# Seven of eight feed-forward blocks: the down projection as seven half-size products (one level of Strassen's identity)

## The chip, the cores and the metric

The kernel runs on one core of a Trainium2 chip. The metric is the time of one execution on the device in microseconds (us). Engines: TensorE (PE; PEld is its weight load), VectorE (DVE), ScalarE (ACT), GpSimd (POOL), and SyncE (SP), whose queue issues the DMAs.

## What is computed

Two layers of a decoder on 1056 tokens (1024 of a prompt, 32 of a sample group), model width 1024, all in FP32. The part that matters here is the feed-forward network at the end of each layer:

```python
hf = einsum('btd,df->btf', rmsnorm(x, norm_ffn_pre), w_up)        # 1024 -> 4096
f  = einsum('btf,fd->btd', square(relu(hf)), w_down)              # 4096 -> 1024
x  = x + rmsnorm(f, norm_ffn_post)
```

Before it stand an input projection, latent attention, chunked spatial gating and an output projection.

## The kernel before, in words

Tokens lie along the free dimension: every activation is a set of tiles of 128 channels x 1056 tokens. A projection is computed in FP32R with both operands split in a high part (rounded to FP32R) and a low part (the remainder), in three passes: high x high, high weights x low activations, low weights x high activations. `dense` (L1660 to L1674) computes one unit of 128 output channels: for each k tile of 128 input channels and each pass, three matmuls of 352 columns, one per group of tokens, into three PSUM banks. Units alternate between banks 0 to 2 and 3 to 5; banks 6 and 7 hold means.

The FFN of a layer runs in FB = 8 blocks of 512 hidden channels. A block has four up units (`up`, 8 k tiles each, 72 matmuls) and eight down units (`down`, and `down_first` for units 0 and 1, whose matmuls stand at L2144; 4 k tiles each, 36 matmuls). Weights come as tiles of 128 x 1024 numbers (512 KB): one for each up unit, one for two down units. The path of a tile is:

- SP loads it into `raw[:, t % 2]` (L559), once the tile two before it has been split (`split`).
- POOL splits it (`split_tile`): L605 writes the high part `wh`, L607 subtracts it and writes the low part `wl`. It waits for `wfree`, by which PE gives a slot back with the first matmul of the next tile. There are two slots.
- PE waits for `split` and runs the tile's matmuls.

The path of the activations in a block: DVE evicts an up unit with relu and the norm's root (L1526), ACT squares it (L1017) and writes the high part `hidh` (L1019), DVE writes the low part `hidl` (L1519). PE's down units read these, and DVE adds each down unit to the running sum in `z[:, m]` (L1552, in the first block a copy, L1550). `acc_full` and `acc_free` tie PE and DVE, `hid_h` and `hid_l` the hidden tiles. Each engine's order is the order of its own program: nothing is scheduled. The first block of a layer and the last stand apart; those between run in a hardware loop.

The last block ends in a special order (L1701), by token groups, so that the norm can begin early.

## Time and profile before

| | us |
|---|---|
| median of 3 runs | 2690.55 (2690.33 to 2691.85) |
| the profiled execution | 2691.78 |
| its span, first to last instruction | 2690.0 |
| PE busy in the span | 2608.7 (97%) |
| DVE busy | 1104.4 (41%) |
| POOL busy | 768.5 (29%) |
| ACT busy | 684.1 (25%) |

Busy time is the time in which an engine has an instruction under way. Matmuls overlap in it: a matmul's recorded duration (some 323 ns for 352 columns) is longer than the spacing of matmuls, which is what their number in a stretch gives. "Idle before" is the time that an engine stood still before the instructions of a group, with what ended it.

### The profile page before, as it was taken

Reading aid. Unit: us, or ns where it says so; the run is one execution under the profiler, and the core shown is the slowest. Engines: PE = TensorE matmul, PEld = TensorE weight load, DVE = VectorE, ACT = ScalarE, POOL = GpSimd, SP = SyncE. Lnnn points to the kernel's source line nnn. Section 1 sums busy time; section 2 is a strip of 40 time slices with the busy share of each in tenths; the row PEclk is TensorE's granted clock in tenths of the full one; section 3 lists DMA queues with packets and bytes.
Section 4 is the critical chain, followed back from the end, with each engine's and each line's share of the span. In section 5 each row is a group of like instructions: output and inputs, shape, how many; then the busy total and the mean of one; then the engine's idle time right before and its main releaser. Section 6 shows DMA issues by size and latency. Waiting matters only on the chain.

```text
span 2690.0 us, 42193 instructions
## 1 busy us (share of the span) xinstructions
PE 2608.7 (97%) x17128; PEld 2363.6 (88%) x17128; DVE 1104.4 (41%) x1519; ACT 684.1 (25%) x1151; POOL 768.5 (29%) x363
## 2 busy tenths in 40 slices
PE   8999999999999999999999999999999999999996
PEld 6995666979999999999879866669799999999996
DVE  5456666254212222322664566652732123212226
ACT  3125555141100110010341255551411000100113
POOL 2431000313334433443114300003043334433440
PEclk9999999999999999999999999999999999999998
DMA  6114222221111111111231242213211111111113
GB/s 220 48 38 128 80 80 72 112 88 40 48 47 47 39 47 47 47 42 44 112 112 40 52 125 81 85 54 120 81 48 48 47 47 41 45 47 47 47 40 137
DMA packets 91492, 185.97 MB, mean 69 GB/s; under 512 B 29664, under 2 KB 42144, under 8 KB 91360
## 3 DMA queue, kind: packets, MB, share of 16 engines
q1 hardware_dynamic: 88656, 175.75, 19.7%
q0 software_dynamic: 2560, 8.39, 1.1%
q8 instruction: 91, 1.49, 0.2%
q14 instruction: 41, 0.34, 0.0%
q10 hardware_dynamic: 144, 0.00, 0.0%
HBM read 157.77 MB, written 23.11 MB: 67 GB/s over the span
## 4 chain that ended last, share of the span: by engine, by line
PE 86%; ACT 4%; DVE 4%; issue 4%; POOLq 1%; DVEq 0%; DMA 0%; POOL 0%; SPq 0%; ACTq 0%
PE psum L1671 54%; PE psum L2144 7%; PE psum L1861 3%; PE psum L1701 3%; PE psum L1887 3%; PE psum L1873 2%; PE psum L1656 2%; PE psum L1764 2%; PE psum L1908 2%; PE psum L1624 1%; ACT z L863 1%; ACT hh L734 1%; PE psum L1921 1%; PE psum L1940 1%; PE psum L1919 1%
## 5 line engine op out<-in xcount | busy, mean ns | idle before, releaser
L605 POOL TENSOR_TENSOR wh<-raw,ones 128x1024 fp32r<-128x1024 f32 x150 | 288.4, 1923 | 1274.3 <-PE psum L1671 1096.3
L1671 PE MATMUL psum<-hh,wh 128*128 128x352 f32 x2064 | 448.6, 325 | 0.0
L1671 PE MATMUL psum<-hh,wl 128*128 128x352 f32 x2064 | 444.8, 323 | 0.0
L1671 PE MATMUL psum<-hl,wh 128*128 128x352 f32 x2064 | 444.3, 323 | 0.0
L607 POOL TENSOR_TENSOR wl<-raw,wh 128x1024 fp32r<-128x1024 f32 x150 | 413.7, 2758 | 21.7
L1017 ACT ACTIVATE z<-z 128x1056 f32<-128x1056 f32 x64 | 69.7, 1089 | 1221.0 <-DVE stat L1530 1199.5
L1671 PEld LDWEIGHTS psum<-hh,wl 128*128 128x128 f32 x2064 | 354.3, 188 | 0.0
L1671 PEld LDWEIGHTS psum<-hh,wh 128*128 128x128 f32 x2064 | 351.8, 189 | 2.5 <-issue 0.6
L1671 PEld LDWEIGHTS psum<-hl,wh 128*128 128x128 f32 x2064 | 350.4, 188 | 0.0
L1526 DVE SCALAR_TENSOR_TENSOR z<-psum,rinv 128x1056 f32<-128x1056 f32 x64 | 80.5, 1258 | 549.6 <-PE psum L1671 542.2
L1552 DVE TENSOR_TENSOR z<-psum,z 128x1056 f32<-128x1056 f32 x104 | 130.8, 1258 | 392.2 <-PE psum L1671 339.3
L1671 PE MATMUL psum<-hidh,wh 128*128 128x352 f32 x1056 | 228.4, 324 | 0.0
L1671 PE MATMUL psum<-hidh,wl 128*128 128x352 f32 x1056 | 227.6, 323 | 0.0
L1671 PE MATMUL psum<-hidl,wh 128*128 128x352 f32 x1056 | 227.4, 323 | 0.0
L1671 PEld LDWEIGHTS psum<-hidh,wl 128*128 128x128 f32 x1056 | 181.4, 188 | 0.0
L1671 PEld LDWEIGHTS psum<-hidh,wh 128*128 128x128 f32 x1056 | 179.9, 189 | 0.0
L1671 PEld LDWEIGHTS psum<-hidl,wh 128*128 128x128 f32 x1056 | 179.3, 188 | 0.0
L628 POOL DMA_INDIRECT z<-cache_k,krows x32 | 30.5, 952 | 395.1 <-DVE cn L1381 390.9
L1519 DVE TENSOR_TENSOR hidl<-z,hidh 128x1056 fp32r<-128x1056 f32 x64 | 129.4, 2022 | 11.9 <-ACT hidh L1019 11.3
L863 ACT ACTIVATE z<-psum,stat 128x128 f32<-128x128 f32 (+7 forms) x128 | 94.7, 740 | 73.0 <-DVE stat L1345 70.5
L1128 DVE TENSOR_TENSOR sacc<-sacc,t 128x1056 f32<-128x1056 f32 x45 | 67.7, 1505 | 104.3 <-ACT t L976 89.7
L1345 DVE TENSOR_REDUCE stat<-psum 128x1 f32<-128x128 f32 (+7 forms) x128 | 95.9, 750 | 14.5 <-PE psum L1864 13.3
(242 smaller groups left out, 3564.8 us busy)
## 6 DMA issues: line engine op xcount, KB each, us to landing
raw<-wst SPq DMA_DIRECT2D x160, 512.0 KB, 3.2
z<-cache_c SPq DMA_DIRECT2D x352, 64.0 KB, 1.8
x<-x_spill SPq DMA_DIRECT2D x4, 4224.0 KB, 14.3
raw<-cache_c SPq DMA_DIRECT2D x160, 64.0 KB, 1.8
x_spill<-x SPq DMA_DIRECT2D x2, 4224.0 KB, 13.4
x_spill<-x SPq DMA_DIRECT2D x6, 1408.0 KB, 5.2
x<-xT SPq DMA_DIRECT2D x8, 528.0 KB, 8.1
yT<-x SPq DMA_DIRECT2D x6, 704.0 KB, 3.3
```

The lines of the kernel that those rows point to most:

```text
L605: pool.tensor_tensor(wh[:, s, :], raw[:, s, :], ones[:, 0:1].to_broadcast([P, TW]), ALU.mult)
L607: pool.tensor_tensor(wl[:, s, :], raw[:, s, :], wh[:, s, :].bitcast(F32), ALU.subtract).then_inc(split.sem, 1)
L863: act.activation(probs[e][:, 0:(j + 1) * P], s_of(e, j), ACT.Exp, bias=stat[:, 32 + e:33 + e], accum_out=stat[:, 36 + e:37 + e]).then_inc( ...
L1345: dve.tensor_reduce(stat[:, 32 + e:33 + e], s_of(e, j), AX.X, ALU.max, negate=True).then_inc(nmax.sem, 1)
L1519: dve.tensor_tensor(hidl[:, j, :], z[:, 10 + j % 2, :], hidh[:, j, :].bitcast(F32), ALU.subtract).then_inc(hid_l.sem, 1)
L1526: dve.scalar_tensor_tensor(out=groups(z[:, 8 + j % 2, :]), in0=acc(j), scalar=0.0, in1=groups(rinv[:, :]), op0=ALU.max, op1=ALU.mult).then ...
L1552: ins = dve.tensor_tensor(groups(z[:, m, :]), acc(m), groups(z[:, m, :]), ALU.add)
L1671: ins = pe.matmul(bank3(u, g), w[:, s, o:o + P], m[:, k, cols(g)], start=(k == 0 and n == 0), stop=(k == kk - 1 and n == 2))
L1701: ins = pe.matmul(bank, u_w[w], m[:, k, cols(g)], start=(first and n == 0), stop=(last and n == 2))
L1861: ins = pe.matmul(ps[2 * e + h][:, 0:w], qs[e][0:KQ, u, tok(j)], keys[0:KQ, 2 * (u % 2) + e, 512 * h:512 * h + w], start=True, stop=not last)
L1887: ins = pe.matmul(ps[6][64 * e:64 * e + 64, 0:P], vals[:, kb, (2 * u + e) * VD:(2 * u + e) * VD + VD], pts[2 * e + kb // 4][:, kb % 4, :], ...
L2144: ins = pe.matmul(bank3(u, g), w[:, 0, o:o + P], m[:, k, cols(g)], start=(k == 0 and n == 0), stop=(k == 3 and n == 2))
```

## The change

In blocks 0 to 6 of each layer the down projection is one level of Strassen's identity. The block's down weights (512 hidden x 1024 output channels) and its hidden activations (512 channels x 1056 tokens) are cut in quarters: 256 hidden channels, 512 output channels, 528 tokens. Seven products of a weight combination with an activation combination take the place of eight products of quarters. The last block stays as it was.

- **PE** (`downs`): for each of seven terms, four units of 128 output channels in the order 0, 3, 1, 2; for each 2 k tiles x 3 passes x 2 halves of 264 columns. Unit u has banks 2u and 2u + 1. The table `TERMS` says for each term which half of the output channels and tokens it goes to, and whether its banks start afresh (terms 0, 2 and 6) or chain on what the term before left in them. DVE adds the banks to `z` after every term, so a chained term goes on from the running combination; each unit of a term waits for the eviction of that unit in the term before (`dn_free`).
- **POOL** (`split_downs`): from the four quarters `a11`, `a12`, `a21`, `a22` it forms four sums and differences (L679, L672) and splits seven operands (L657, L659). The quarters lie in `t0`, `cn`, `sacc` and `t1`, and `s4` in the cosine table, all free in the FFN.
- **SP** (`downs_in`): eight transfers of 256 KB take the place of four of 512 KB; they wait for the last split of the block before. The cosine table is loaded anew during the last block of the first layer.
- **ACT and DVE** (`hidden_parts`, `parts_of`): ACT squares in place; DVE forms four differences of quarters (`less`, L1667); the high and low parts are made per quarter combination into four tiles of `hidh` and `hidl` (L1674), three of which are written a second time in a block. DVE evicts 28 half-size units (`take`, L1688 and L1690).

The core of the diff:

```diff
+SB = FB - 1
+N_UP, N_DN = 4, 7
+HB, HW = TOK // 2, TOK // 4
+TURN = (0, 3, 1, 2)
+TERMS = [(1, 3, True, (1, 1)), (2, 3, False, (0, 1)), (0, 0, True, (0, 0)), (3, 1, False, (0, 1)),
+         (1, 1, False, (1, 1)), (2, 1, False, (1, 0)), (0, 0, True, (0, 0))]
...
+                def downs_in(tile):
+
+                    for n, (left, right) in enumerate(((a11, a12), (a11, a12), (a21, a22), (a21, a22))):
+                        own = slice(TW // 2 * (n % 2), TW // 2 * (n % 2) + TW // 2)
+                        for j, slot in enumerate((left, right)):
+                            sp.dma_start(slot[:, own],
+                                         wst[l, tile + n][:, TW // 2 * j:TW // 2 * j + TW // 2]).then_inc(dn_in.sem, 16)
...
+                def split_downs(s):
+
+                    at.step(dn_in, 128)
+                    pool.wait_ge(dn_in.sem, at.value(dn_in))
+                    pool.tensor_tensor(a21, a21, a22, ALU.add)
+                    pool.drain()
+                    split_one(s, a21)
+                    combine(a21, a21, a11, ALU.subtract)
+                    combine(s4, a12, a21, ALU.subtract)
+                    split_one(1 - s, s4)
+                    split_one(s, a11)
+                    split_one(1 - s, a21)
+                    combine(a21, a22, a21, ALU.subtract)
+                    split_one(s, a21)
+                    split_one(1 - s, a22)
+                    split_one(s, a12)
...
+                def hidden_parts():
+
+                    squared(0)
+                    squared(1)
+                    act.drain()
+                    high_hid(0, slice(0, 2), b11)
+                    high_sum(1, 0, b12)
+                    for k in range(2):
+                        squared(2 + k)
+                        act.drain()
+                        high_hid(2, slice(k, k + 1), b22)
+                    high_sum(3, 0, b12)
+                    high_sum(1, 4, b11)
+                    high_sum(2, 8, b12)
+                    act.wait_ge(dn_full.sem, at.value(dn_full, 12))
+                    high_hid(0, slice(0, 2), b21)
...
+                    def take(f, units):
+
+                        for u in units:
+                            at.step(dn_full)
+                            dve.wait_ge(dn_full.sem, at.value(dn_full))
+                            outs_of = [TERMS[f][3]]
+                            for i, half in outs_of:
+                                part = quarter(4 * i + u, half)
+                                if first and (i, half, u) not in seen:
+                                    ins = dve.tensor_copy(part, dn_banks(u))
+                                else:
+                                    ins = dve.tensor_tensor(part, dn_banks(u), part, ALU.add)
+                                seen.add((i, half, u))
+                            ins.then_inc(dn_free.sem, 1)
+
+                    both = slice(0, 2)
+                    relu(0)
+                    relu(1)
...
+                    squares_done(2)
+                    less(b12, b12, b11)
+                    low(0, both, b11)
+                    low(1, both, b12)
+                    relu(2)
+                    low(2, slice(0, 1), b22)
+                    relu(3)
+                    low(2, slice(1, 2), b22)
+                    take(0, TURN[:2])
+                    squares_done(2)
+                    less(b12, b22, b12)
+                    take(0, TURN[2:])
+                    low(3, both, b12)
+                    take(1, TURN[:2])
+                    dve.drain()
+                    less(b11, b12, b11)
+                    take(1, TURN[2:])
+                    low(1, both, b11)
+                    take(2, TURN[:2])
+                    dve.drain()
+                    less(b12, b21, b12)
+                    take(2, TURN[2:])
+                    low(2, both, b12)
+                    take(3, TURN)
+                    low(0, both, b21)
+                    for f in range(4, 7):
+                        take(f, TURN)
...
+                def downs(flip):
+
+                    ready = (2, 4, 1, 5, 6, 7, 8)
+                    where = (1, 2, 0, 3, 1, 2, 0)
+                    for f in range(7):
+                        s, t, fresh = (f + flip) % 2, where[f], TERMS[f][2]
+                        take_tile()
+                        pe.wait_ge(hid_l.sem, at.value(hid_l, ready[f]))
+                        for u in TURN:
+                            if f:
+                                pe.wait_ge(dn_free.sem, at.value(dn_free, -3))
+                            elif u < 2:
+                                pe.wait_ge(acc_free.sem, at.value(acc_free, u - 1))
+                            at.step(dn_free)
+                            for k in range(2):
+                                o = u // 2 * 4 * P + k * 2 * P + u % 2 * P
+                                for n, (w, m) in enumerate(((wh, hidh), (wh, hidl), (wl, hidh))):
+                                    for q in range(2):
+                                        ins = pe.matmul(psum[:, 2 * u + q, 0:HW], w[:, s, o:o + P],
+                                                        m[:, t, k * HB + q * HW:k * HB + q * HW + HW],
+                                                        start=(fresh and k == 0 and n == 0), stop=(k == 1 and n == 2),
+                                                        skip_group_check=True)
+                                        release(ins)
+                            ins.then_inc(dn_full.sem, 1)
```

How the instructions stand, at the two places that matter. First VectorE, in the first block of a layer, from the last up unit's low half on. Before (`hidl` low parts, L1526 the relu, L1550 the evictions of the eight down units):

```order
L1519 TENSOR_TENSOR hidl<-z,hidh 128x1056 [waits hid_h]
L1526 SCALAR_TENSOR_TENSOR z<-psum,rinv 128x1056 [waits acc_full]
L1530 MEMSET stat 128x1
L1519 TENSOR_TENSOR hidl<-z,hidh 128x1056 [waits hid_h] x2
L1550 COPY z<-psum 128x1056 [waits acc_full] x8
```

After, the same place up to the end of the fourth term's evictions:

```order
L1674 TENSOR_TENSOR hidl<-z,hidh 128x528 [waits hid_h]
L1688 COPY z<-psum 128x528 [waits dn_full] x2
L1667 TENSOR_TENSOR z<-z 128x2x528 [waits h_sq]
L1688 COPY z<-psum 128x528 [waits dn_full] x2
L1674 TENSOR_TENSOR hidl<-z,hidh 128x1056 [waits hid_h]
L1688 COPY z<-psum 128x528 [waits dn_full] x2
L1667 TENSOR_TENSOR z<-z 128x2x528
L1688 COPY z<-psum 128x528 [waits dn_full] x2
L1674 TENSOR_TENSOR hidl<-z,hidh 128x1056 [waits hid_h]
```

The low parts and the differences now stand between the evictions for which PE waits; before, all low parts stood ahead of them.

Second GpSimd, in a block between the first and the last. Before (one tile of the loop; the down tiles are split in the same way):

```order
L603 ISA [waits raw_in0]
L605 TENSOR_TENSOR wh<-raw,ones 128x1024 [waits wfree]
L607 TENSOR_TENSOR wl<-raw,wh 128x1024
```

After, from the sum of two quarters to the split of the third operand (`t` is t0 or t1, `cos` holds `s4`):

```order
L679 TENSOR_TENSOR sacc<-sacc,t 128x1024 [waits dn_in]
L655 REGISTER_ALU
L657 TENSOR_TENSOR wh<-sacc,ones 128x1024 [waits wfree]
L659 TENSOR_TENSOR wl<-sacc,wh 128x1024
L672 TENSOR_TENSOR sacc<-sacc,t 128x1024
L672 TENSOR_TENSOR cos<-cn,sacc 128x1024
L655 REGISTER_ALU
L657 TENSOR_TENSOR wh<-cos,ones 128x1024 [waits wfree]
L659 TENSOR_TENSOR wl<-cos,wh 128x1024
L655 REGISTER_ALU
L657 TENSOR_TENSOR wh<-t,ones 128x1024 [waits wfree]
L659 TENSOR_TENSOR wl<-t,wh 128x1024
```

Sums and differences stand between the splits, on the same engine.

## Rows read from the trace of the kernel before

**Rows 1.** The page, busy us (share of the span) and instructions of each engine:

```profile
PE 2608.7 (97%) x17128; PEld 2363.6 (88%) x17128; DVE 1104.4 (41%) x1519; ACT 684.1 (25%) x1151; POOL 768.5 (29%) x363
```

**Rows 2.** Busy time by stretch, two FFN blocks; columns as in the first line:

```profile
core 0: us, PE busy (x) PEld busy (x) DVE busy (x) ACT busy (x) POOL busy (x), PEclk, DMA share, GB/s
1192.28:1285.47 93.19, 93.19 (x578) 93.19 (x577) 23.47 (x20) 8.72 (x8) 36.85 (x16) 1.00 0.13 45
1965.53:2058.72 93.19, 93.19 (x577) 93.19 (x577) 23.45 (x20) 8.71 (x8) 36.86 (x16) 1.00 0.13 46
```

**Rows 3.** The chain of waits: start us, us, what:

```profile
633.12 11.62 PE psum L2144 x72
644.74 81.57 PE psum L1671 x504
```

**Rows 4.** Waits, 633 to 1285 us: who waited for whom, us, times, longest:

```profile
POOL wh L605 <- PE psum L1671: 341.5, 49, 7.2
DVE z L1526 <- PE psum L1671: 262.4, 28, 10.4
```

**Rows 5.** PE groups by shape, FP32 matmuls of attention: busy us, mean ns:

```profile
L1861 PE MATMUL psum<-scratch,free_b 96*128 96x512 f32 x96 | 48.8, 593 | 0.0
...
L1861 PE MATMUL psum<-scratch,free_a 96*128 96x384 f32 x32 | 13.0, 486 | 0.0
...
L1861 PE MATMUL psum<-scratch,free_a 96*128 96x256 f32 x32 | 9.6, 380 | 0.0
...
L1861 PE MATMUL psum<-scratch,free_b 96*128 96x128 f32 x32 | 6.3, 277 | 0.0
```

**Rows 6.** PEld groups by shape, weight loads of 128 and 32 columns:

```profile
L1671 PEld LDWEIGHTS psum<-hidh,wl 128*128 128x128 f32 x1056 | 181.4, 188 | 0.0
...
L1919 PEld LDWEIGHTS psum<-z,sacc 128*32 128x32 f32 x256 | 5.0, 108 | 5.4 <-issue 4.1
```

**Rows 7.** Timeline of PE around an FP32R matmul of 128 columns (L1864):

```profile
271.68 0.39 PE L1861 MATMUL psum<-scratch,free_a 96*128 96x128 f32 x2
271.82 0.31 PE L1864 MATMUL psum<-trir,idr 128*128 128x128 f32 x1
271.96 0.52 PE L1908 MATMUL psum<-cst,z 128*128 128x128 f32 x3
```

**Rows 8.** DVE groups by shape, whole span, the last row for 633 to 1297 us:

```profile
L1552 DVE TENSOR_TENSOR z<-psum,z 128x1056 f32<-128x1056 f32 x104 | 130.8, 1258 | 392.2 <-PE psum L1671 339.3 <-PE psum L2144 52.9
...
L1374 DVE COPY z<-psum 128x512 f32<-128x512 f32 x32 | 22.0, 689 | 5.9 <-PE psum L1908 5.8
...
L1576 DVE TENSOR_TENSOR z<-psum,z 128x704 f32<-128x704 f32 x12 | 10.7, 890 | 8.3 <-PE psum L1701 8.3
...
L1519 DVE TENSOR_TENSOR hidl<-z,hidh 128x1056 fp32r<-128x1056 f32 x30 | 61.6, 2053 | 4.6 <-ACT hidh L1019 4.3
```

**Rows 9.** Timeline of DVE and POOL after the last up unit:

```profile
634.54 1.83 DVE L1519 TENSOR_TENSOR hidl<-z,hidh 128x1056 fp32r<-128x1056 f32 x1
636.91 2.83 DVE L1519 TENSOR_TENSOR hidl<-z,hidh 128x1056 fp32r<-128x1056 f32 x1 [0.54 <-ACT hidh L1019]
...
633.36 1.90 POOL L605 TENSOR_TENSOR wh<-raw,ones 128x1024 fp32r<-128x1024 f32 x1 [6.39 <-PE psum L2144]
635.40 3.23 POOL L607 TENSOR_TENSOR wl<-raw,wh 128x1024 fp32r<-128x1024 f32 x1
```

**Rows 10.** ACT groups by shape: the square, and a high part of 512 elements:

```profile
L1017 ACT ACTIVATE z<-z 128x1056 f32<-128x1056 f32 x64 | 69.7, 1089 | 1221.0 <-DVE stat L1530 1199.5 <-DVE hl L1163 21.5
...
L817 ACT ACTIVATE hh<-z 128x512 fp32r<-128x512 f32 x16 | 10.0, 627 | 18.4 <-POOL z L623 18.4
```

**Rows 11.** Timeline of POOL, a split with DVE elsewhere:

```profile
644.98 1.90 POOL L605 TENSOR_TENSOR wh<-raw,ones 128x1024 fp32r<-128x1024 f32 x1 [6.36 <-PE psum L1671]
647.02 2.40 POOL L607 TENSOR_TENSOR wl<-raw,wh 128x1024 fp32r<-128x1024 f32 x1
```

**Rows 12.** DMA issues: times, KB each, median us to landing:

```profile
raw<-wst SPq DMA_DIRECT2D x160, 512.0 KB, 3.2
```

More of the change, by code:

```diff
@@ new lines, in _ @@
+                at.step(split)
+                sp.wait_ge(root_full.sem, at.whole(root_full, 7))
+                downs_in(base + 4)
+                at.step(split, N_DN)
+                with sp.Fori(0, SB // 2) as i:
+                    at.enter(i, {split: 2 * (N_UP + N_DN)})
+                    for b in range(2):
+                        tile = i * 16 + (base + 8 + 8 * b)
+                        for j in range(2):
+                            up_in(tile + j, j, j - 8)
+                        sp.wait_ge(split.sem, at.value(split))
+                        downs_in(tile + 4)
+                        for j in range(2, 4):
+                            up_in(tile + j, j, j - 1)
+                        at.step(split, N_UP + N_DN)
+                    at.leave(SB // 2)
@@ L569, in _ @@
                 if l < DEPTH - 1:
-                    sp.wait_ge(hid_l.sem, at.whole(hid_l, 4 * FB))
+                    sp.wait_ge(hid_l.sem, at.whole(hid_l, hid_l.per))
                     for u in range(2):
@@ L666, in _ @@
                 taken_elsewhere()
-                split_tiles(TILES_LAYER - T_OUT - KD - 6)
+                at.step(split)
+                at.step(wfree)
+                split_downs(1)
+                with pool.Fori(0, SB // 2) as i:
+                    at.enter(i, {split: 22, wfree: 22, raw_in[0]: 64, raw_in[1]: 64, dn_in: 256})
+                    for b in range(2):
+                        for j in range(4):
+                            split_tile(j % 2, slot=(j + b) % 2)
+                        split_downs(b)
+                    at.leave(SB // 2)
+                split_tiles(6)
                 split_tile(0)
@@ L1516, in low, with block_of @@
+                def block_of(last):
                     def low(j):
@@ L1531, in block_of @@
                         at.step(act_new)
-                        if first and j == 1:
-                            low_h(range(EARLY, KD), gn[:, G_FFN_PRE:G_FFN_PRE + KD])
-                            low_w(1, at.whole(w_hi, 4))
-                            dve.drain()
                         if j > 0:
```

204 lines of the change are left out of this document (138 added, 66 removed).

## Prediction

> **What bounds the kernel now.** I read the page's shares first. TensorE is busy for 97% of the span, VectorE for 41%, GpSimd for 29% and ScalarE for 25% [rows 1]. Shares are means over stages, so the stretch that the change touches came next. Two FFN blocks, one of each layer, each take 93.19 us, PE busy in all of it, at a granted clock of 1.00, which is 2.4 GHz [rows 2]. The reader is to see there that PE never waits within a block, while POOL needs 36.9 us and DVE 23.4 us of it. The chain of waits says the same from the other side: for a whole block it names only matmuls of the dense loop and of the first down units [rows 3]. A block has 4 x 72 + 8 x 36 = 576 matmuls of 352 columns, so one costs 93.19 / 576 = 161.8 ns. The waits of the other engines confirm the direction: POOL waited 341.5 us for PE to give back a weight slot, and DVE 262.4 us for full accumulators [rows 4]. So only less PE time, or a new PE wait, can move the total. Seven blocks in each of two layers change: 14 blocks, and 1 us in a block is worth 14 us.
>
> **What PE saves.** The eight down units of a block go: 288 x 161.8 ns = 46.6 us. In their place stand seven products of 4 units x 2 k x 3 passes x 2 column halves = 48 matmuls of 264 columns, 336 in all. No row has a matmul of this type with 264 columns, so I bound it. In proportion to columns it costs 161.8 x 264 / 352 = 121.4 ns. If only the streaming part shrinks, at one column per cycle of 2.4 GHz (the granted clock is 1.00), 88 columns save 36.7 ns, which leaves 125.1 ns. That durations follow columns is seen in the plain FP32 matmuls of attention: 593, 486, 380 and 277 ns for 512, 384, 256 and 128 columns [rows 5], some 0.83 ns per column, which is two passes at 0.42. Against it stands that every matmul loads its own 128 x 128 weights. Loads of 128 and of 32 columns are recorded at 188 and 108 ns [rows 6], so 96 columns are worth 80 ns and 128 some 107 ns, just under the 110 ns that 264 columns stream. And around the one FP32R matmul of 128 columns, the next matmul begins 0.14 us after it [rows 7], so neither its stream nor its load holds the array for 162 ns. I take 123 ns: 41.3 us for the seven products, and 5.3 us less than before. The ends, 40.8 and 42.0 us, stay in the range.
>
> The Trainium skill, "TensorE: Matmul & The Clock Gate", section on the back-to-back issue gap, has a warm gap of N/2.4 + 2.5 ns. It gives 149 ns for 352 columns, which the trace contradicts (161.8 ns). By it 264 columns would take 112.5 ns, and the seven products 37.8 us.
>
> **What VectorE adds.** Evictions from PSUM grow from 8 of 1056 elements (1258 ns) to 28 of 528. Rows of 512 and 704 elements read 689 and 890 ns [rows 8], so one takes 0.71 us: 10.1 us become 19.8. New are four sums or differences of squared activations, and the low halves become seven of 1056 elements instead of four. The eviction reads one tensor from SBUF and never lengthens (1258 ns mean over 104). The low half reads two, and lengthens: 1.83 and 2.83 us [rows 9]. The reader is to lay its times beside POOL's. The first runs 634.54 to 636.37, POOL's product held 633.36 to 635.26: 1.11 us from there. The second ends 639.74, POOL's subtraction 638.63: 1.11 us again. POOL's subtraction started at 635.40 and took 3.23 us, where undisturbed ones take 2.40. So these operations exclude one another, each for its whole length. DVE's cost is 1.11 us plus what is left of POOL's operation.
>
> In the products of index 0, 1 and 2 DVE does four evictions (2.8 us), one difference and one low half (2 x 1.11 = 2.2 us), and waits twice for POOL. The waits are 0 at best and a full 1.72 us, as in the second case above, at worst. POOL's split holds 4.3 us of each 5.9 us product, so a random arrival waits 0.73 x 1.08 = 0.8 us. With 0.2 us of drains and hops a stage costs 2.8 + 2.2 + 1.6 + 0.2 = 6.8 us against PE's 48 x 123 ns = 5.9 us. PE cannot run ahead: unit u of a product waits for the eviction of unit u of the one before, because both chain in the same banks. Nor is there much slack at entry. After the last up unit DVE's relu takes 1.26 us, ACT's square and half-size copy 1.09 + 0.6 [rows 10], DVE's half-size low 0.6 + 0.8, hops 0.4: the first eviction ends at 5.5 us, and PE wants that bank at 5.9. So PE waits 3 x 0.9 - 0.4 = 2.3 us, and each of some five restarts exposes a weight load of 0.11 us: 2.9 us. I take 3.2, since POOL's margin, next, is thin. With no lock wait it is 0; with a full one each time it is near 3 x 2.7 = 8 us.
>
> **What GpSimd adds.** A split costs 1.90 + 2.40 us with a gap of 0.14 between them, 4.45 us [rows 11]. There were 8 in a block, now there are 11, and four sums of 2.4 us with a drain: 37 us become about 59, of some 91. It is hidden in the up units, where PE spends 11.6 us per tile. Among the products it is tight. From the start of the last up unit to the end of the last split POOL has 7 splits (31.2 us), three differences (7.7 us), and DVE's operations of two inputs in its way (7 to 8 x 1.11 = 8 us): 46.9 us. PE needs the last split after 11.6 + 6 x 5.9 = 47.0 us, and its own waits for DVE give POOL some 3 us more. I cost POOL at nothing on that ground.
>
> **Other edits.** ACT gains about 4 us per block on 8.7 and idles otherwise. DMA moves the same bytes: the down tiles come as eight transfers of 256 KB, issued on the SP queue after the last split of the block before. A tile of 512 KB lands in 3.2 us [rows 12]; four of them have over 20 us before POOL needs them, and the up tiles queued behind them over 10 us more. In the first block they start after the reciprocal root and have the two up units of 23.3 us. The cosine table's reload is hidden by the last block. The new order of the slots costs nothing.
>
> **The sum.** A block: 46.6 + 41.3 + 3.2 = 91.1 us against 93.2, 2.1 us less, times 14 = 29 us. The profiled execution took 2691.78 us (span 2690.0 and 1.8 around it), so it would take 2662.4; the median of the runs shown, 2690.55, lies 1.2 lower. Forecast: **2661 us**. Its own range is 2637 to 2680, for waits of 1.5 to 4.5 us in a block.
>
> **Rivals.**
> *Full gain.* DVE meets POOL rarely, since it can slip into POOL's drains; a stage then costs 5.3 us, under PE's 5.9. Block 87.9 us, 5.3 x 14 = 74 us less: 2616 us. For it: the lock lets DVE in after each POOL operation. Against: the 30 low halves of seven blocks take 2053 ns in the mean [rows 8], 0.9 us over 1.11, with POOL busy for 37 us of a block and not 59.
> *GpSimd becomes the bound (slower).* The place is the last split among the products. Each DVE operation costs POOL up to 1.11 us, and each POOL operation costs DVE the same; a late split also delays the next unit's eviction, so that the waits add up instead of overlapping. If POOL is 4 us late in a block besides the 3.2, the block is 95.1 us: 27 us more, 2717 us. It decides from 5.3 us of waits in all. For it: 46.9 us of work in a window of 47.0. Against: PE's waits for DVE widen that window.
> *A matmul of 264 columns costs what one of 352 does.* Something fixed per matmul, the weight load with its handover, sets the 161.8 ns. Then the products take 54.4 us, the waits vanish, a block is 101.0 us: 109 us more, 2800 us. The point of decision is 139 ns, 46.6 us / 336. Against: [rows 5 to 7]. For: nothing here has this type at 264 columns, and 161.8 is 15 ns above 352 columns at 2.4 GHz, unexplained.
> The same section of the skill's TensorE page has a sustained gap of about 81 ns at 128 columns and 131 ns at 512, 0.13 ns per column. By it 88 columns save 11 ns only, a product's matmul costs 150 ns, and the result is 2745 us; no row here bears it out, and rows 5 speak against it.
> That the change does less than it says I leave out: the instruction order has the 336 matmuls of 264 columns.
>
> **How the numbers follow.** Forecast 0.59, full gain 0.13, GpSimd 0.20, fixed matmul cost 0.08. About 0.2% (5 us) is what a measurement of this kernel can tell from no change. Of the forecast's case 0.05 falls within it. Faster: 0.54 + 0.13 = 0.67; same 0.05; slower 0.28. The range leaves out the fixed cost, a tail above the GpSimd case and a little below the full gain: 2614 to 2725.
>
> **What would show it.** Right: matmuls of 264 columns spaced 121 to 125 ns; in each block PE waits for DVE's evictions, mostly in the products of index 1 to 4, and hardly in 5 and 6; DVE's two-input operations at 1.9 us and more in the mean; POOL's subtraction often over 2.4 us. Wrong: waits of PE for POOL's split above 1 us per block (the slower rival), no waits (full gain), a spacing above 139 ns, or a wait for a DMA at the sum of the two left quarters.

## The result, and the profile after

| | before | after |
|---|---|---|
| median, us | 2691.07 (4 runs) | 2716.24 (4 runs, 2711.61 to 2721.42) |
| the profiled execution | 2691.78 | 2716.44 |
| its span | 2690.0 | 2714.6 |

The change makes the kernel slower by 0.9%: the ratio is 1.0093, 95% interval 1.0081 to 1.0105. The forecast was 2661 us. The page of the changed kernel, busy us (share) and instructions, against [rows 1]:

```profile
PE 2557.4 (94%) x17800; PEld 2301.6 (85%) x17800; DVE 1451.4 (53%) x1911; ACT 730.5 (27%) x1207; POOL 1141.3 (42%) x503
```

PE has 51 us less to do and the span is 25 us longer. So PE stands still, or goes slower, where it did neither before. Two whole blocks, one of each layer, as in [rows 2]:

```profile
core 0: us, PE busy (x) PEld busy (x) DVE busy (x) ACT busy (x) POOL busy (x), PEclk, DMA share, GB/s
1154.83:1247.14 92.31, 88.52 (x627) 87.69 (x625) 47.98 (x48) 12.07 (x12) 62.96 (x26) 1.00 0.11 36
2021.57:2113.88 92.31, 88.48 (x626) 87.65 (x625) 47.98 (x48) 12.06 (x12) 62.95 (x26) 1.00 0.15 47
```

These blocks are faster than 93.19 us, but by 0.88 us only: if all fourteen were like them, 14 x 0.88 = 12.3 us in all. The profiled execution is 24.7 us slower, so 37 us have to be explained by what such an undisturbed block does not show. What PE waited for (waiting engine and line, releaser, us in total, times, longest):

```profile
PE psum L2360 <- POOL wl L659: 51.4, 36, 2.7
PE psum L1879 <- issue: 20.6, 6, 4.9
```

The first row is a wait within the block: products (L2360) for a split by GpSimd (L659). The second is new in kind: at up units (L1879) PE stood still six times for 20.6 us, and no tile was late. [Rows 3] of before have neither. For VectorE's evictions, where the prediction looked for the waits, PE waited twice, 1.1 us.

**Within the block.** The chain of waits from 1200 to 1230 us, the stretch from the last up unit to the end of product 3, by line:

```profile
by line: POOLq L658 32.9%; POOL wl L659 26.5%; POOLq L673 18.9%; issue 16.6%; POOLq L671 10.9%; PE psum L2360 1.7%; POOLq L655 0.5%
```

It is GpSimd's. Its timeline there (start us, us, line, operation; in brackets its idle time and who ended it):

```profile
1201.80 1.90 POOL L657 TENSOR_TENSOR wh<-cos,ones 128x1024 fp32r<-128x1024 f32 x1 [1.76 <-PE psum L2360]
1203.84 2.40 POOL L659 TENSOR_TENSOR wl<-cos,wh 128x1024 fp32r<-128x1024 f32 x1
1207.95 3.01 POOL L657 TENSOR_TENSOR wh<-t,ones 128x1024 fp32r<-128x1024 f32 x1 [1.71 <-PE psum L2360]
1211.10 3.22 POOL L659 TENSOR_TENSOR wl<-t,wh 128x1024 fp32r<-128x1024 f32 x1
1215.01 2.18 POOL L657 TENSOR_TENSOR wh<-sacc,ones 128x1024 fp32r<-128x1024 f32 x1 [0.69 <-PE psum L2360]
1217.33 3.24 POOL L659 TENSOR_TENSOR wl<-sacc,wh 128x1024 fp32r<-128x1024 f32 x1
1220.73 3.24 POOL L672 TENSOR_TENSOR sacc<-t,sacc 128x1024 f32<-128x1024 f32 x1 [0.16 <-issue]
1224.17 2.66 POOL L657 TENSOR_TENSOR wh<-sacc,ones 128x1024 fp32r<-128x1024 f32 x1 [0.20 <-issue]
1226.98 2.34 POOL L659 TENSOR_TENSOR wl<-sacc,wh 128x1024 fp32r<-128x1024 f32 x1
```

Two things are to be seen. GpSimd is idle for 1.76, 1.71 and 0.69 us, each time until PE begins another product: there are two slots, and a split may not begin before PE has left one. And of the seven operations that follow the first two, six are longer than in [rows 11]: 3.01, 2.18 and 2.66 for 1.90 us, 3.22 and twice 3.24 for 2.40 us, where VectorE's two-input operations fall beside them. So the split for product 2 begins behind PE's start of product 1 and takes 6.4 us, where a product takes 5.8. The split for product 4 stands behind a difference, and ends at 1229.32. The timeline of PE has the first matmuls of products 2 and 4:

```profile
1214.55 0.51 PE L2360 MATMUL psum<-hidh,wh 128*128 128x264 f32 x2 [0.95 <-POOL wl L659]
...
1229.54 0.51 PE L2360 MATMUL psum<-hidh,wh 128*128 128x264 f32 x2 [2.66 <-POOL wl L659]
```

VectorE's two-input groups and evictions by shape (busy us, mean ns), against [rows 8]:

```profile
L1690 DVE TENSOR_TENSOR z<-psum,z 128x528 f32<-128x528 f32 x360 | 244.4, 701 | 137.7 <-PE psum L2360 133.6 <-issue 3.9
...
L1674 DVE TENSOR_TENSOR hidl<-z,hidh 128x1056 fp32r<-128x1056 f32 x84 | 174.5, 2091 | 2.2 <-issue 2.0
L1667 DVE TENSOR_TENSOR z<-z 128x1056 f32<-128x1056 f32 x56 | 117.5, 2097 | 18.4 <-ACT z L1117 15.9
```

The evictions wait 133.6 us for PE, not PE for them. Their rhythm in product 6 gives the price of a matmul (timeline of DVE):

```profile
1240.06 0.71 DVE L1690 TENSOR_TENSOR z<-psum,z 128x528 f32<-128x528 f32 x1 [0.75 <-PE psum L2360]
...
1247.34 0.71 DVE L1690 TENSOR_TENSOR z<-psum,z 128x528 f32<-128x528 f32 x1 [0.75 <-PE psum L2360]
```

Five units of 12 matmuls in 7.28 us: 121.3 ns, in proportion to the columns. Seven products would take 40.8 us; from 1201.43 to 1247.14 they take 45.7 us. So 4.9 us of the block are waits and restarts. PE's waits for GpSimd's splits are 51.4 / 14 = 3.7 us of them.

**At the jump.** PE's hardware loop (L2414) holds two blocks now: a block has 4 + 7 = 11 tiles, an odd number, so the two slots change places from one block to the next. The loop runs three times and jumps back twice per layer. The timeline of PE and of SP's queue around one jump:

```profile
865.04 0.40 PE L2360 MATMUL psum<-hidh,wl 128*128 128x264 f32 x2
...
870.31 1.24 PE L1879 MATMUL psum<-hh,wh 128*128 128x352 f32 x3 [4.87 <-issue]
...
858.62 0.33 SPq L592 DMA_DIRECT2D t<-wst  x1
...
863.39 0.33 SPq L592 DMA_DIRECT2D t<-wst  x1
864.44 11.54 SPq L585 DMA_DIRECT2D raw<-wst  x2
```

And busy time by stretch, columns as above:

```profile
865.20:870.30 5.10, 0.25 (x3) 0.03 (x1) 0.71 (x1) 0.00 (x0) 0.00 (x0) 0.97 0.73 249
...
846.10:849.50 3.40, 3.25 (x15) 3.25 (x16) 1.25 (x2) 0.00 (x0) 2.44 (x2) 0.50 0.00 0
849.60:853.00 3.40, 3.40 (x30) 3.40 (x29) 1.74 (x3) 0.00 (x0) 1.84 (x1) 1.00 0.00 0
...
869.97:873.37 3.40, 3.06 (x10) 3.06 (x11) 0.00 (x0) 0.00 (x0) 2.18 (x2) 0.50 0.04 11
```

The first row is the pause: PE has nothing, while the DMA engines are busy for 0.73 of it, mostly with the transfers of the down tiles. The six pauses of the row above are one at each of the four jumps (4.9, 4.4, 4.4 and 4.6 us) and a second one some 3 us behind the last two (1.6 and 0.8 us). The fetch of instructions goes on throughout the loop. From 650 to 1250 us the instruction queue moved, in the kernel before (packets, MB, share):

```profile
q8 instruction: 7, 0.11, 0.1%
```

And in the changed one:

```profile
q8 instruction: 36, 0.59, 0.4%
```

The other rows of the stretches show the third loss. In 3.40 us behind a wait at product 4, and in 3.40 us behind the pause, the granted clock is 0.50, the 1.2 GHz level: 15 matmuls where the next stretch at 1.00 has 30, so up to 1.7 us each. The fourteen blocks of this execution have ten stretches at half clock, 44 us in all, those of before none. What they cost can be read from whole blocks: from 2261.51 to 2355.34 and from 2456.15 to 2549.97 us stand two blocks with one stretch of 3.4 us and no pause, and they take 93.83 and 93.82 us where undisturbed ones take 92.31. That is 1.5 us each, so some 20 us for 44 us at half clock.

The sum of the profiled execution, read block by block: the fourteen blocks together take 28.2 us more than fourteen of 93.19 us, and the rest of the kernel 3.6 us less than before. The 28.2 us are -12.3 us from the faster products, +20.6 us from the pauses at the jump, and 19.9 us that are left for the half clock, and agree with the price just read. Outside the blocks the half clock stood for some 15 us less than before, which can account for the 3.6 us.

### The profile page after: what moved, and what is told of

Read it like the earlier page. It is cut to its first block, busy times and chain, and to the rows that moved or that the text cites. A ratio compares the mean times of both kernels' runs of the same rounds, so it can differ in the third digit from the quotient of the medians.

```text
span 2714.6 us, 44972 instructions
## 1 busy us (share of the span) xinstructions
PE 2557.4 (94%) x17800; PEld 2301.6 (85%) x17800; DVE 1451.4 (53%) x1911; ACT 730.5 (27%) x1207; POOL 1141.3 (42%) x503
## 4 chain that ended last, share of the span: by engine, by line
PE 37%; issue 26%; POOLq 21%; POOL 7%; ACT 3%; DVE 3%; DMA 1%; SPq 1%; DVEq 0%; ACTq 0%
PE psum L1879 13%; POOLq L658 12%; POOL wl L659 7%; POOLq L673 4%; PE psum L2069 3%; POOLq L671 3%; PE psum L2095 3%; PE psum L2081 2%; PE psum L1909 2%; POOLq L680 2%; PE psum L1864 2%; PE psum L1972 2%; PE psum L2116 2%; PE psum L2360 1%; PE psum L1832 1%
## 5 line engine op out<-in xcount | busy, mean ns | idle before, releaser
L1879 PE MATMUL psum<-hh,wh 128*128 128x352 f32 x2064 | 452.4, 328 | 18.2 <-issue 18.2
L657 POOL TENSOR_TENSOR wh<-raw,ones 128x1024 fp32r<-128x1024 f32 x94 | 182.1, 1937 | 651.2 <-PE psum L1879 542.6
L1879 PE MATMUL psum<-hh,wl 128*128 128x352 f32 x2064 | 447.9, 325 | 2.4 <-issue 2.4
L1879 PE MATMUL psum<-hl,wh 128*128 128x352 f32 x2064 | 446.9, 325 | 0.0
L2360 PE MATMUL psum<-hidh,wh 128*128 128x264 f32 x1568 | 328.3, 291 | 53.9 <-POOL wl L659 51.4
L1879 PEld LDWEIGHTS psum<-hh,wh 128*128 128x128 f32 x2064 | 354.4, 190 | 21.2 <-issue 19.0
L1879 PEld LDWEIGHTS psum<-hh,wl 128*128 128x128 f32 x2064 | 356.5, 189 | 3.3 <-issue 3.3
L1879 PEld LDWEIGHTS psum<-hl,wh 128*128 128x128 f32 x2064 | 352.8, 189 | 0.0
L2360 PE MATMUL psum<-hidl,wh 128*128 128x264 f32 x1568 | 322.1, 287 | 0.0
L2360 PE MATMUL psum<-hidh,wl 128*128 128x264 f32 x1568 | 321.9, 287 | 0.0
L1690 DVE TENSOR_TENSOR z<-psum,z 128x528 f32<-128x528 f32 x360 | 244.4, 701 | 137.7 <-PE psum L2360 133.6
L2360 PEld LDWEIGHTS psum<-hidh,wh 128*128 128x128 f32 x1568 | 246.9, 192 | 65.6 <-issue 54.2
L1674 DVE TENSOR_TENSOR hidl<-z,hidh 128x1056 fp32r<-128x1056 f32 (+1 forms) x112 | 227.5, 2041 | 54.9 <-ACT hidh L1121 52.7
L659 POOL TENSOR_TENSOR wl<-raw,wh 128x1024 fp32r<-128x1024 f32 x94 | 246.1, 2618 | 13.4
L2360 PEld LDWEIGHTS psum<-hidl,wh 128*128 128x128 f32 x1568 | 246.7, 192 | 0.0
L2360 PEld LDWEIGHTS psum<-hidh,wl 128*128 128x128 f32 x1568 | 246.5, 191 | 0.0
L1121 ACT ACTIVATE hidh<-z 128x1056 fp32r<-128x1056 f32 (+1 forms) x112 | 107.9, 976 | 235.8 <-DVE z L1667 232.0
L1667 DVE TENSOR_TENSOR z<-z 128x1056 f32<-128x1056 f32 x56 | 117.5, 2097 | 18.4 <-ACT z L1117 15.9
```

The source lines that it names most:

```text
L657: pool.tensor_tensor(wh[:, s, :], src, ones[:, 0:1].to_broadcast([P, TW]), ALU.mult)
L659: pool.tensor_tensor(wl[:, s, :], src, wh[:, s, :].bitcast(F32), ALU.subtract).then_inc(split.sem, 1)
L1121: act.activation(hid_of(t, hidh)[:, ks, :], src[:, ks, :], ACT.Copy).then_inc(hid_h.sem, 1)
L1667: dve.tensor_tensor(out, one, two, ALU.subtract).then_inc(h_sum.sem, 1)
L1674: dve.tensor_tensor(hid_of(t, hidl)[:, ks, :], src[:, ks, :], hid_of(t, hidh)[:, ks, :].bitcast(F32), ALU.subtract).then_inc(hid_l.sem, 1)
L1690: ins = dve.tensor_tensor(part, dn_banks(u), part, ALU.add)
```

## The experiments

Theory A: the pauses belong to PE's jump back. Theory B: the splits are late through the two slots, the serial difference and VectorE's hold on GpSimd, all together.

**1. PE's loop written out.**

```diff
-                with pe.Fori(1, 1 + SB // 2) as i:
...
-                    for b in range(2):
-                        ups(b)
-                        downs(b)
...
+                for b in range(SB - 1):
+                    ups(b % 2)
+                    downs(b % 2)
```

> The change, with PE's three loop passes of two blocks written out, all other engines as they are. Theory A (the loop body of two blocks, some 2500 instructions, no longer stays in the instruction memory, so each jump back waits for code): the four pauses at the jumps (4.9, 4.4, 4.4 and 4.6 us, and two follow-ups of 2.0 and 1.1 us) vanish, 21 us, and with them about six of the 3.4 us stretches at the half clock that follow, some 10 us: near 2685 us. Rival A2 (PE waits there for the first up tile, for POOL or a DMA): the pauses stay, 2716 us. Both: POOL's waits at the products of index 2, 3 and 4 stay.

Measured: 2684.08 us (10 runs), ratio to before 0.9972 [0.9961, 0.9983]. Busy time in a block:

```profile
769.49:861.62 92.13, 88.48 (x627) 87.66 (x626) 47.98 (x48) 12.07 (x12) 63.21 (x26) 1.00 0.14 46
```

The row of its waits for the split:

```profile
PE psum L2360 <- POOL wl L659: 48.2, 33, 2.7
```

The waits for the split stay; the row of pauses at up units is gone, and theory A's 2685 us is met. The fetch is not gone: from 650 to 1250 us the instruction queue still moved 0.52 MB, and PE waited for none of it. So it is the jump that exposes a fetch, not the amount of code. The jump was worth 32 us, more than the 20.6 us that it shows by itself. In this profiled execution (2679.32 us, the second fastest of the ten) only one half-clock stretch of 3.4 us stands in each layer's blocks, though the waits at product 4 are still there, and the fourteen blocks together are 37.7 us shorter: 20.6 us of pauses and 17 us of clock. Not all of this is the jump's doing. The ten executions differ among themselves, from 2677.35 us at a mean granted clock of 0.992 to 2692.17 us at 0.986. At that same 0.986 the kernel with the jump took 2711.61 and 2716.44 us, some 22 us more, about the pauses. Without the jump the change is already a small gain.

**2. The third difference made in the up units.** The first difference, which the third is formed from, gets a place of its own (`s5`) in the sine table, which is loaded anew for the second layer as the cosine table is. So the third can be formed at once, and no longer stands between two splits.

```diff
+                    combine(s5, a21, a11, ALU.subtract)
+                    split_one(s, a21)
+                    combine(s4, a12, s5, ALU.subtract)
+                    pool.tensor_tensor(a21, a22, s5, ALU.subtract)
                     pool.drain()
-                    split_one(s, a21)
-                    combine(a21, a21, a11, ALU.subtract)
-                    combine(s4, a12, a21, ALU.subtract)
...
-                    split_one(1 - s, a21)
-                    combine(a21, a22, a21, ALU.subtract)
+                    split_one(1 - s, s5)
```

> The change, with the third difference of weights formed during the up units (one more buffer, the sine table, reloaded like the cosine table). Theory B (PE waits 2.8 us at index 4 because POOL forms a difference between two splits there, with only two slots to run ahead in): that wait goes in all 14 blocks, 39 us, and the half clock stretches behind it, some 10 us more: 2665 to 2680 us. Rival B2 (POOL's queue as a whole is too long, by the operations of DVE that it excludes): the wait only moves to the next products and the time stays above 2705 us.

Measured: 2676.84 us (4 runs), ratio 0.9945 [0.9929, 0.9962]. What PE waited for:

```profile
PE psum L1881 <- issue: 18.1, 6, 4.6
PE psum L2362 <- POOL wl L661: 17.3, 24, 2.2
```

The waits for splits fell from 51.4 to 17.3 us; the pauses are nearly unchanged (20.6 to 18.1 us). So the two losses are separate, and the serial difference carried most of the first. Rival B2, by which the time would have stayed above 2705 us, is out.

**3. Both edits.**

> Both edits together. If they are independent the gains add: about 30 + 45 us off 2716, so 2635 to 2650 us, below the kernel before. If one pause hid the other: 2665 us or more.

Measured: 2644.43 us (4 runs), ratio 0.982 [0.98, 0.984]: faster than both kernels. Busy time in a block:

```profile
680.50:770.13 89.63, 88.45 (x627) 87.64 (x625) 49.19 (x48) 12.07 (x12) 64.70 (x26) 1.00 0.16 50
```

And the timeline of GpSimd and PE at product 2, the largest wait left in such a block:

```profile
733.68 2.95 POOL L659 TENSOR_TENSOR wh<-t,ones 128x1024 fp32r<-128x1024 f32 x1 [1.77 <-PE psum L2362]
736.77 3.21 POOL L661 TENSOR_TENSOR wl<-t,wh 128x1024 fp32r<-128x1024 f32 x1
740.03 0.51 PE L2362 MATMUL psum<-hidh,wh 128*128 128x264 f32 x2 [0.73 <-POOL wl L661]
```

One split, that for product 2, is still too long by VectorE's share.

**4. The kernel before with a loop of two blocks.** Nothing of the change, only the long loop body.

```diff
-                with pe.Fori(1, FB - 1) as i:
+                with pe.Fori(1, FB // 2) as i:
...
+                    for b in range(2):
...
```

> The kernel before, with nothing changed but PE's loop: three passes of two blocks in place of six of one (1152 matmuls and their weight loads in the body). Theory A: two pauses of 4 to 5 us per layer at the jumps back, and the half clock behind them: 2691 + 20 to 30 = 2711 to 2721 us. Rival A2 (the pause has to do with tiles and not with code): 2691 us, no pause.

Measured: 2694.2 us (10 runs), ratio 1.0014 [1.0004, 1.0023]. The instruction queue from 650 to 1250 us:

```profile
q8 instruction: 35, 0.57, 0.4%
```

PE's timeline at the jump, and below it the busy time of the pause:

```profile
866.04 0.74 PE L1671 MATMUL psum<-hh,wh 128*128 128x352 f32 x3 [1.01 <-issue]
```

```profile
865.00:866.04 1.04, 0.03 (x2) 0.01 (x1) 0.98 (x1) 0.00 (x0) 0.00 (x0) 1.00 0.00 0
```

The fetch of 0.57 MB comes with the body of two blocks, and so does a pause at each of the four jumps, but of 1.0, 1.3, 0.7 and 0.9 us, and there is no half clock behind them. Theory A's 2711 to 2721 us was missed, and A2's "no pause" too: the pause of 4.9 us needs something more. Here the DMA share is 0.00 during the pause, and 0.73 there. This is theory C: the fetch stands behind the down tiles.

**5. The down tiles issued later.**

```diff
-                        sp.wait_ge(split.sem, at.value(split))
-                        downs_in(tile + 4)
                         for j in range(2, 4):
                             up_in(tile + j, j, j - 1)
+                        downs_in(tile + 4)
```

> The changed kernel with its loop, but SP issues the eight transfers of the down tiles (2 MB) behind the up tiles of index 2 and 3, which wait for two further splits, so some 5 us after PE's jump back instead of 0 to 5 us before it. Theory C (at the jump PE's instructions are fetched by DMA, and the fetch stands behind the 2 MB of down tiles): the four pauses of PE at the jump shrink from 4.7 us to the 1.2 to 1.5 us that the kernel before shows with a loop of two blocks, 3.3 us each, 13 us in all, and the stretches at half clock behind them (some 1.5 us each) go too: 2696 to 2704 us, after 2716. Rival (the pause is the cost of fetching a long body, whatever else moves): pauses stay at 4.7 us, 2716 us. The tiles are needed more than 20 us later, so no new wait for them.

Measured: 2709.92 us (4 runs), ratio 1.0065 [1.0049, 1.0082]. Waits of PE:

```profile
PE psum L1878 <- issue: 9.8, 5, 2.4
```

PE's timeline at the first jump, and below it the busy time of the pause:

```profile
868.32 0.74 PE L1878 MATMUL psum<-hh,wh 128*128 128x352 f32 x3 [2.05 <-issue]
```

```profile
866.20:868.30 2.10, 0.07 (x1) 0.00 (x0) 0.71 (x1) 0.00 (x0) 0.00 (x0) 1.00 0.74 242
```

The row has the pauses go from 20.6 to 9.8 us. It leaves one out, since the trace puts the 1.5 us at the second jump down to VectorE (L1689); with it they are 11.3 us, so what the DMA engines carry does lengthen them. They did not come down to 1.0 us: an up tile of 512 KB is on its way there instead, with the same share of 0.74 for a shorter time. The run gained 6 us where theory C had 12 to 20. Part of that is clock: the profiled execution (2715.25 us) is the slowest of the four, at 0.982, with more half-clock stretches in its blocks than before the edit, though the waits at product 4 had not changed (51.5 us). The two executions at 0.986 took 2706.55 and 2706.63 us, 5 to 10 us less than those of the changed kernel at the same clock, and that fits the 9.3 us of pauses. Theory C is right in direction, and its number was too high by twofold or more.

The times of the instruction queue's 16 KB packets show the mechanism directly. At the first jump of the changed kernel PE ends its work at 865.45 us; the packet goes from 867.60 to 868.52, and PE resumes at 870.31. In experiment 5 PE ends at 866.27, the packet goes from 865.09 to 866.47, and PE resumes at 868.32. In experiment 4 PE ends at 865.03, the packet goes from 863.11 to 864.33, and PE resumes at 866.04. At all twelve jumps of these three runs PE resumes 1.6 to 1.9 us after the end of a packet, also at the two where the trace names VectorE. What differs is when the last packet starts: 1.5 to 2.0 us before PE runs dry with idle DMA engines, 1.2 us before in experiment 5, and 0.9 to 2.2 us after it in the changed kernel.

**6. VectorE quiet.** Loop written out, and in blocks 1 to 6 of each layer three differences and three low halves among the products replaced by a memset of one column.

```diff
+                    def less0(out, one, two):
...
+                        dve.memset(stat[:, 26:27], 0.0).then_inc(h_sum.sem, 1)
...
-                    less(b12, b22, b12)
+                    less0(b12, b22, b12)
                     take(0, TURN[2:])
-                    low(3, both, b12)
+                    low0(3, both, b12)
...
```

> The changed kernel with PE's loop written out, and in blocks 1 to 6 of each layer VectorE's three differences and three low halves among the products of index 0 to 3 left out (a memset of one column gives each semaphore); this part of the computation is missing, the instructions of PE, GpSimd and the evictions are all there. Theory B (GpSimd's splits are late at index 2, 3 and 4 because of two things together: a split may not start before PE takes the tile before the last, and VectorE's two-input operations hold GpSimd for 1.1 us each): without VectorE's operations a split is 4.45 us of 5.8 us, and the split, the difference and the next split end 11.5 us behind the start of product 2, where PE wants them at 11.6: all of the 4.3 us of waits of a block go, block 88.0 us in place of 92.1, 12 x 4.1 = 49 us, 2630 to 2642 us against 2684 with the loop written out. Rival B2 (the slots and the serial difference alone): the wait at index 4 stays at 2 us or more, and the result is 2655 us or above.

Measured: 2633.68 us (4 runs), ratio 0.9787 [0.977, 0.9803], against 0.9972 in experiment 1. Busy time in a block:

```profile
724.18:812.72 88.54, 88.20 (x626) 87.62 (x625) 37.32 (x48) 12.19 (x12) 59.15 (x26) 1.00 0.15 48
```

The timeline of GpSimd and PE, with the difference in its old place ahead of the split for product 4:

```profile
741.19 2.40 POOL L672 TENSOR_TENSOR sacc<-t,sacc 128x1024 f32<-128x1024 f32 x1 [0.16 <-issue]
743.79 1.90 POOL L657 TENSOR_TENSOR wh<-sacc,ones 128x1024 fp32r<-128x1024 f32 x1 [0.20 <-issue]
745.83 2.39 POOL L659 TENSOR_TENSOR wl<-sacc,wh 128x1024 fp32r<-128x1024 f32 x1
...
748.27 0.51 PE L2374 MATMUL psum<-hidh,wh 128*128 128x264 f32 x2 [0.21 <-POOL wl L659]
```

The kernel leaves out this part of the computation; the instructions of PE and GpSimd are all there. Up to the split for product 4 every operation of GpSimd has its undisturbed length, and product 4 waits 0.21 us in place of 2.66. The block is 3.6 us shorter than in experiment 1, 43 us over twelve blocks of the 50 measured. So the slots and the serial difference leave GpSimd just enough time, and VectorE's operations take it away: either cure, this or experiment 2, removes the wait at product 4. This experiment's rival B2, the slots and the difference alone, is out.

**7 and 8. VectorE's operations spread out.** Experiment 3 with one two-input operation in each of products 0 to 2, and the rest in 3 to 5; then with those for products 4 and 5 earlier by one eviction.

```diff
                     take(0, TURN[2:])
-                    low(3, both, b12)
                     take(1, TURN[:2])
-                    dve.drain()
-                    less(b11, b12, b11)
+                    low(3, both, b12)
                     take(1, TURN[2:])
-                    low(1, both, b11)
                     take(2, TURN[:2])
                     dve.drain()
-                    less(b12, b21, b12)
+                    less(b11, b12, b11)
...
```

> The version with both edits (loop written out, third difference made early: 2644 us) with VectorE's two-input operations moved from two in each of the products 0, 1 and 2 to one in each of 0, 1 and 2, and the rest in 3 to 5. Theory B: the split for product 2 meets one such operation and ends within 5.6 us of 5.8, the wait of 1.0 us at index 2 goes, 14 x 1.0 = 14 us at most: 2630 to 2638 us. Rival (the wait at index 2 comes from the two GpSimd operations that the splits for 1 and 2 stand behind, not from VectorE): 2644 us, wait unchanged. Risk: a new wait at index 4 or 5 for VectorE's late low half.

> As the version with VectorE's operations spread (2645 us), but the low half for product 4 begins behind the first eviction of product 3 and the difference behind it before the last one, so that ScalarE's copy and VectorE's low half for product 5 end some 1.5 us earlier. There that low half ended at 758.07 and PE, which could have begun product 5 near 757.0, began at 758.16. Theory B (a term waits for whichever comes last, GpSimd's split or VectorE's low half, and both fit if no product holds more than about one two-input operation and a half): the 1.1 us at index 5 goes and none comes in its place at index 4: block 88.4 to 88.9 us after 89.7, 2628 to 2636 us. Rival (VectorE and GpSimd together have no room left and the wait only moves on): 2643 to 2648 us.

Measured: 2645.04 us (4 runs), ratio 0.9826 [0.981, 0.9843], and 2642.51 us (5 runs), ratio 0.9819 [0.9806, 0.9833]. Neither differs from experiment 3, and both forecasts of theory B (2630 to 2638 and 2628 to 2636 us) were missed. The timeline of the first version around product 5:

```profile
756.09 1.98 DVE L1676 TENSOR_TENSOR hidl<-z,hidh 128x1056 fp32r<-128x1056 f32 x1
...
758.16 0.48 PE L2366 MATMUL psum<-hidh,wh 128*128 128x264 f32 x2 [0.86 <-issue]
```

The second version, busy time in a block:

```profile
672.94:762.61 89.67, 88.63 (x627) 87.77 (x625) 52.38 (x48) 12.07 (x12) 61.75 (x26) 1.00 0.15 48
```

The low halves of VectorE as a group (busy us, mean ns):

```profile
L1676 DVE TENSOR_TENSOR hidl<-z,hidh 128x1056 fp32r<-128x1056 f32 x84 | 227.6, 2722 | 2.2 <-issue 2.0
```

And its timeline at product 5:

```profile
748.52 1.98 DVE L1676 TENSOR_TENSOR hidl<-z,hidh 128x1056 fp32r<-128x1056 f32 x1
...
750.60 0.48 PE L2367 MATMUL psum<-hidh,wh 128*128 128x264 f32 x2 [0.83 <-issue]
```

The wait at product 2 went, as theory B said, and one of the same size came at product 5, for VectorE's low half (750.50, 0.1 us before PE goes on; the wait is named "issue"). That low half was the risk named ahead of experiment 7. Setting it earlier did not help. GpSimd's time in a block fell from 64.70 to 61.75 us, and VectorE's rose from 49.19 to 52.38 us, with the low half at 2722 ns: the same waiting, now on the other engine. The rival of experiment 8 held.

**9. Late tiles without a jump.** Experiment 8 with the edit of experiment 5.

> The version before with the down tiles issued later, as in the run that kept PE's loop. Theory C (the burst of down tiles costs only where it meets the fetch of PE's instructions at the jump back): here is no jump, so no change against the version with the burst at its old place, within 3 us. Rival (the burst slows something else too, such as the up tiles or GpSimd): 5 us or more less than it.

Measured: 2642.59 us (5 runs), ratio 0.9818 [0.9805, 0.9832]: the same as experiment 8. Moving the burst helps only where there is a jump for it to meet.

## Why the prediction was wrong

**What bounds the kernel: right, but for the clock.** PE's time and its new waits moved the total, and with them PE's clock, which the prediction took as 1.00 throughout.

**The price of a matmul: right.** 123 ns were taken, 121.3 ns measured, at the proportional end. The rival of a fixed cost per matmul is out. So are both estimates that the prediction worked out from figures of the Trainium skill ("TensorE: Matmul & The Clock Gate", section on the back-to-back issue gap): 112.5 ns is too low here, 150 ns too high.

**VectorE: price about right, place wrong.** Evictions take 0.70 us (0.71 forecast), two-input operations 2.09 us in the mean ("1.9 us and more"). But PE does not wait for them: a stage of VectorE takes 6.2 us, in place of 6.8, and is hidden behind GpSimd's longer one. The exclusion of the two engines cost PE time through GpSimd's split, not through an eviction.

**GpSimd: the first failed step, within the block.** "I cost POOL at nothing on that ground" rested on 46.9 us of work in a window of 47.0 us, from the last up unit to the last split. That balance holds only if work can be done ahead anywhere in the window. It can't: each split is held until PE leaves a slot, and the trace shows 4.2 us of GpSimd idle ahead of the splits for products 1 to 3. The bound had to be drawn per product: a split of 4.45 us in 5.8 us leaves room for one VectorE operation of 1.11 us, and product 2 met two; the splits for products 3 and 4, with the difference between them, are 11.6 us of work in 11.6 us (experiment 6), with no room for any. PE's waits and restarts are 4.9 us per block where 3.2 were forecast: (92.3 - 91.1) x 14 = 17 us of the error. One of the four sums, that of the two left quarters (L679), takes 3.4 us in place of 2.4, but in the up units, where it is hidden. The prediction's own sign for the late splits, waits for POOL's split above 1 us per block, was met with 3.7. This is the slower rival's mechanism, in another place: it put the late split at the end of the products, and it is at 2 and 4. Its 2717 us are near the measurement, but its block of 95.1 us is not: 92.3 us were measured.

**The order of the slots: the second failed step, and the larger one.** "The new order of the slots costs nothing" put at nothing, without a reason, the edit that makes PE's loop body two blocks long; no part of the prediction has the jump or the clock. In the profiled execution they cost 20.6 us of pauses and 19.9 us of half clock. With the 17 us of the block, and 3.6 us that the rest of the kernel saves, that makes 54 of the 55 us between forecast and result. Taking the jump away gives 32 of them back, and "Own range 2637 to 2680" then misses by 4 us. The DMA term was wrong with it: "DMA moves the same bytes" is true, and the eight transfers land in time, but they are issued in one burst just where PE fetches its code.

The Trainium skill has a rule that bears on this step, in "Runtime: NRT & Kernel Launch", section on instruction fetch mechanics, and the prediction missed it: PE's instruction memory holds 2048 instructions and is refilled in blocks of 16 KB, 256 instructions each, and a taken branch whose target is not in the current window of two such pages has to fetch it by DMA before execution goes on. By the counts of matmuls and weight loads alone the old body has 2 x 576 = 1152 instructions, that of experiment 4 2304, and the new one 2 x 2 x 624 = 2496. The traces agree with the size of the memory: 0.11 MB fetched with the old body, 0.57 MB and more with the long ones, and a pause at the jump with those only. They do not agree with a window of two pages: 1152 instructions are more than that too, and the old loop jumps back without a pause.

**ACT and the reloads: right** at nothing; neither is among the new waits of PE.

**Where the expected gain went.** 5.8 us of PE time leave each block. 4.9 us come back: 3.7 us as waits for GpSimd's splits, the rest at the restarts of PE from product to product (1.1 us remain in experiment 6, where the products take 41.9 us). Pauses and clock take more than what is left. Of the 14 x 5.8 = 81 us the version with both edits keeps 48, 1.8% of the time.

**Open.** Which waits are followed by a half-clock stretch: the same waits of 2.6 us at product 4 had one in some blocks and none in others, and in experiment 1's trace none in the twelve blocks behind the first of each layer. Executions of one kernel differ in this as well. So the price of such a stretch is measured, but how many a change brings is not foretold by anything here, and how much of the 19.9 us the jump causes stays open. How far a pause at the jump would shrink with no data transfer at all beside it was not tried for the changed kernel; 0.7 to 1.3 us are from the kernel before.

## What to carry to other kernels

Between a producer and a consumer with two slots, make the balance per item and not over the window: the time from the release of a slot to its next use, against the producer's work including all that stands in its queue and what another engine can take from it. When an edit lengthens a hardware loop's body, count its instructions, look in the trace for a pause at the jump back and for a fetch beside it, and keep bursts of data away from there, or write the loop out. Fetches alone are no sign of a loss: the loop written out had as many and no pause. Where two engines exclude each other, moving operations about within the tight stretch only moved the wait (experiments 7 and 8); taking one out of the stretch altogether helped (experiment 2).

## What the runs showed of the hardware

- A PE loop of one block fetched 0.11 MB of instructions from 650 to 1250 us, one of two blocks 0.57 to 0.59 MB. The same two blocks written out fetched 0.52 MB, and PE never paused for it. At the jump back of the long body PE stood still for 0.7 to 1.3 us with the DMA engines idle, 1.5 to 2.4 us with a 512 KB tile under way, and 4.4 to 4.9 us behind 2 MB of tiles. It resumed 1.6 to 1.9 us after the end of a 16 KB packet of the instruction queue each time.
- After such a pause, and after some waits of 2.6 us, the granted clock was 0.50; a stretch of 3.4 us of it made a block 1.5 us longer (93.83 for 92.31 us). Before the change nothing of the kind stood in these blocks.
- VectorE's operations of two inputs from SBUF and GpSimd's exclude one another in both directions: GpSimd's subtraction takes 2.40 us alone and 3.2 us beside VectorE, VectorE's low half between 1.25 and 3.45 us for the same work (all 84 of the changed kernel).
